# Projection steps between the RWKV chain's products: counts per place, order of the items, and the place of one sigmoid

## What is computed

```python
# per layer
x += 1/2 * g0 * RMSNorm_post(SwiGLU_a(mod0(RMSNorm_pre(x))))
x +=       g1 * RMSNorm_post(HybridMixer(mod1(RMSNorm_pre(x))))
x += 1/2 * g2 * RMSNorm_post(SwiGLU_b(mod2(RMSNorm_pre(x))))

# HybridMixer: h @ w_in gives the columns of three branches and of the merge gates
def rwkv_step(state, inp):                  # 16 heads of 64, forward and backward in time
    sa = einsum("bhij,bhj->bhi", state, a_t)
    state = state * w_t[:, :, None, :] + sa[..., None] * b_t[:, :, None, :] + v_t[..., None] * k_t[:, :, None, :]
    return state, einsum("bhij,bhj->bhi", state, r_t)

def mamba(z, xbc, dt):
    xbc = silu(depthwise_conv_centred(xbc, conv_w) + conv_b)      # 5 taps, 3072 channels
    ...                                                          # chunked scan gives y
    y = y * silu(z)                                              # 2048 channels

def diff_attention(q, k, v): ...
```

## Time and profile before

| what | value |
|---|---|
| median of 3 runs | 2737.57 us (2735.68 to 2737.82) |
| the profiled execution's own time | 2737.22 us |
| its span | 2735.5 us |
| mean granted TensorE clock | 0.993 |
| PE busy | 2620.0 us (96%) |
| DVE busy | 1413.6 us (52%) |
| ACT busy | 499.4 us (18%) |
| POOL busy | 232.0 us (8%) |

### The profile page before, as it was taken

How to read it: one execution, slowest core, us unless ns; L and a number is a source line. 1 busy time by engine, 2 the same in 40 slices (tenths; PEclk the granted TensorE clock), 3 DMA queues, 4 the chain that set the end, 5 groups by cost and what they waited for, 6 DMA issues and landing times.

```text
span 2735.5 us, 66483 instructions
## 1 busy us (share of the span) xinstructions
PE 2620.0 (96%) x30077; PEld 1906.3 (70%) x30077; DVE 1413.6 (52%) x2560; ACT 499.4 (18%) x1016; POOL 232.0 (8%) x372
## 2 busy tenths in 40 slices
PE   6999999999999999999999999999999899999999
PEld 6777877777775555577787778777778745546776
DVE  3552465677775856312035425456787768562001
ACT  1000223122222332100010011322222223221000
POOL 6000102000001101100000010110000011100000
PEclk9999999999999999999999999999999999999999
DMA  9894433322327542484469734423222275424452
GB/s 364 309 337 151 133 117 123 111 83 92 116 80 239 169 168 94 144 291 165 157 242 340 271 128 142 152 91 113 87 83 88 91 253 191 143 96 154 138 168 93
DMA packets 226348, 445.12 MB, mean 163 GB/s; under 512 B 7545, under 2 KB 102327, under 8 KB 226065
## 3 DMA queue, kind: packets, MB, share of 16 engines
q1 hardware_dynamic: 211376, 395.59, 41.5%
q0 software_dynamic: 12960, 38.98, 4.5%
q10 hardware_dynamic: 1728, 6.29, 0.6%
HBM read 422.88 MB, written 17.96 MB: 161 GB/s over the span
## 4 chain that ended last, share of the span: by engine, by line
PE 81%; DVE 11%; ACT 3%; issue 2%; DMA 2%; POOL 1%; DVEq 0%; ACTq 0%; SPq 0%; POOLq 0%
PE ps L1039 79%; DVE scratch L2228 5%; DVE scratch L2231 2%; DVE scratch L2234 1%; DVE gbc L2234 1%; PE ps L1068 1%; DVE scratch L2544 1%; DMA scratch<-in_ada_w 1%; DMA ring<-in_w_in 1%; DMA scratch<-acs_scratch 0%; DMA acs_scratch<-scratch 0%; ACT scratch L2053 0%; ACT scratch L2051 0%; ACT scratch L2200 0%; DVE x L2234 0%
## 5 line engine op out<-in xcount | busy, mean ns | idle before, releaser
L1039 PE MATMUL ps<-hT,ring 64*64 64x256 f32 (+3 forms) x9472 | 1147.9, 367 | 8.3 <-issue 3.1
L1039 PEld LDWEIGHTS ps<-hT,ring 64*64 64x64 f32 (+2 forms) x9472 | 943.0, 160 | 155.9 <-issue 35.8
L1039 PE MATMUL ps<-scratch 64*64 64x32 f32 (+6 forms) x15264 | 846.7, 255 | 56.8 <-DVE scratch L2228 16.1
L1039 PEld LDWEIGHTS ps<-scratch 64*64 64x64 f32 (+2 forms) x15264 | 592.6, 140 | 332.3 <-issue 206.2
L2228 DVE TENSOR_TENSOR scratch<-scratch,ps 128x256 f32<-128x256 f32 (+3 forms) x314 | 155.2, 494 | 661.1 <-ACT scratch L1895 533.1
L1039 PE MATMUL ps<-ring,hT 64*64 64x256 f32 (+2 forms) x2816 | 425.4, 421 | 5.3 <-DVE scratch L2234 2.6
L1039 PEld LDWEIGHTS ps<-ring,hT 64*64 64x64 f32 (+1 forms) x2816 | 228.7, 149 | 143.3 <-issue 116.8
L2228 DVE TENSOR_TENSOR scratch<-scratch 128x512 f32<-128x512 f32 (+4 forms) x426 | 276.1, 648 | 75.4 <-ACTq L2035 31.8
L1039 PE MATMUL ps<-ring,scratch 128*128 128x512 f32 x512 | 234.7, 593 | 0.5
L2234 DVE SCALAR_TENSOR_TENSOR scratch<-scratch,ccol 128x1024 f32<-128x1024 f32 x120 | 154.2, 1285 | 15.2 <-DMA scratch<-in_ada_w 11.3
L1895 ACT ACTIVATE scratch<-ps 128x512 f32<-128x512 f32 x40 | 23.9, 597 | 746.1 <-PE ps L1039 746.1
(11 more groups left out here) (228 smaller groups left out, 1392.8 us busy)
## 6 DMA issues: line engine op xcount, KB each, us to landing
ring<-in_w_in SPq DMA_DIRECT2D x56, 2048.0 KB, 9.0
ring<-in_ffn_w SPq DMA_DIRECT2D x88, 1024.0 KB, 9.0
scratch<-in_ada_w SPq DMA_DIRECT2D x35, 2048.0 KB, 16.2
scratch<-in_ffn_w SPq DMA_DIRECT2D x44, 1024.0 KB, 5.0
ring<-in_w_branch_mamba SPq DMA_DIRECT2D x8, 2048.0 KB, 8.0
scratch<-acs_scratch POOLq DMA_DIRECT2D x24, 512.0 KB, 5.8
scratch<-fill_scratch SPq DMA_DIRECT2D x16, 512.0 KB, 8.7
ring<-in_w_branch_rwkv SPq DMA_DIRECT2D x4, 2048.0 KB, 11.1
```

The lines of the kernel that those rows point to most:

```text
L1039: return pe.matmul(o, lhsT, rhs, start=start, stop=stop)
```

## The change

1. `FILL` has another order. z3 moves from fourth to fifth place, and c1 to c4 each come ahead of a q item that they stood behind; the last three stay.
2. `FILL_PAIR` has new counts. The total is the same 448; the rows' sums are 51, 48, 55, 57, 54, 64, 58 and 61.
3. Convolution 0 belongs to pair 1, not 2. In pair 1 its 16 taps stand otherwise than elsewhere: none before `pair_finish` and none behind the first half, 4 behind the second, 3 in each of four levels. Pair 2 has no taps and no `conv_product`.
4. ACT visits the fill at point `lv` too. At `k3`, if an item ends there, `conv_sigmoid` of the complete convolution goes right behind the item's two copies, ahead of its opens; if not, it stands alone as before.
5. POOL's product for z3 moves from the turn q = 2 to q = 3, one turn later in its loop; the waits for `silu_product` go by the new order (`silu_order`).

```diff
-FILL = [("z", 0), ("z", 1), ("z", 2), ("z", 3), ("c", 0), ("q", 0), ("c", 1), ("q", 1), ("c", 2), ("q", 2),
-        ("c", 3), ("q", 3), ("c", 4), ("c", 5), ("v", 0), ("v", 1)]
+FILL = [("z", 0), ("z", 1), ("z", 2), ("c", 0), ("z", 3), ("c", 1), ("q", 0), ("c", 2), ("q", 1), ("c", 3),
+        ("q", 2), ("c", 4), ("q", 3), ("c", 5), ("v", 0), ("v", 1)]
...
 FILL_POINTS = ("ops", "mid", "lv", "k0", "k1", "k2", "k3", "r0", "u0", "s1", "r1", "u1", "s2", "r2", "u2", "s3", "r3", "u3", "end")
-FILL_PAIR = ((8, 8, 8, 2, 2, 2, 2, 0, 2, 0, 1, 1, 4, 1, 2, 0, 2, 2, 3),
-             (14, 10, 10, 3, 3, 3, 3, 0, 2, 0, 1, 1, 4, 1, 2, 0, 2, 2, 3),
-             (14, 10, 10, 3, 3, 3, 3, 0, 2, 0, 1, 1, 4, 1, 2, 0, 2, 2, 3),
-             (14, 10, 10, 3, 3, 3, 3, 0, 2, 0, 1, 1, 4, 1, 2, 0, 2, 2, 3),
-             (14, 8, 7, 1, 2, 2, 2, 0, 1, 0, 1, 1, 3, 1, 1, 0, 1, 1, 3),
-             (11, 8, 8, 2, 2, 2, 2, 0, 2, 0, 1, 2, 4, 2, 2, 0, 2, 2, 9),
-             (8, 8, 8, 2, 2, 2, 2, 0, 2, 0, 1, 1, 4, 1, 2, 0, 2, 2, 3),
-             (14, 8, 7, 1, 2, 2, 2, 0, 1, 0, 1, 1, 3, 1, 1, 0, 1, 1, 0))
+FILL_PAIR = ((7, 9, 9, 1, 2, 2, 2, 0, 2, 0, 1, 2, 6, 1, 2, 0, 2, 1, 2),
+             (13, 8, 8, 0, 0, 1, 1, 0, 1, 0, 1, 1, 6, 1, 2, 0, 1, 1, 3),
+             (13, 7, 8, 1, 1, 1, 1, 0, 2, 0, 2, 2, 7, 1, 2, 0, 2, 2, 3),
+             (13, 9, 9, 1, 2, 2, 2, 0, 2, 0, 1, 2, 6, 1, 2, 0, 2, 1, 2),
+             (13, 8, 8, 0, 0, 1, 1, 0, 1, 0, 1, 1, 6, 1, 2, 0, 1, 1, 9),
+             (13, 10, 8, 1, 1, 1, 1, 0, 2, 0, 2, 2, 7, 1, 2, 0, 2, 2, 9),
+             (13, 10, 8, 1, 1, 1, 1, 0, 2, 0, 2, 2, 7, 1, 2, 0, 2, 2, 3),
+             (13, 7, 8, 1, 1, 1, 1, 0, 2, 0, 2, 2, 7, 2, 2, 0, 2, 2, 8))
...
-CONV_AT_LEVELS = CONV_SIGMOID = {2: 0, 3: 1, 4: 2, 5: 3, 6: 4, 7: 5}
+CONV_AT_LEVELS = CONV_SIGMOID = {1: 0, 3: 1, 4: 2, 5: 3, 6: 4, 7: 5}
...
-                    if q == 2:
+                    if q == 3:
                         store_product("z", 3)
...
                     act.wait_ge(*fill_evac(l, 2 * i + 2))
+                    if between is not None:
+                        conv_sigmoid(between)
...
                             item_evacuate(u // 2, conv)
                             evacuated_units[0] += 2
+                            conv = None
+                    if conv is not None:
+                        conv_sigmoid(conv)
...
                     if q:
-                        fill_evacuations(q - 1, "k3")
-                        if q - 1 in CONV_SIGMOID:
-                            conv_sigmoid(CONV_SIGMOID[q - 1])
+                        fill_evacuations(q - 1, "lv")
+                        fill_evacuations(q - 1, "k3", CONV_SIGMOID.get(q - 1))
                         fill_evacuations(q - 1, "u0")
...
-                            convolve(2 if d else 4)
+                            convolve((4 if d else 0) if p == 1 else (2 if d else 4))
...
-                            convolve(2)
+                            convolve(3 if p == 1 else 2)
```

More of the change, by code:

```diff
@@ L1975, in fill_evacuate, with item_evacuate @@
                             sigmoid_from_tanh(zsig, silu_sig)
-                def item_evacuate(i):
+                def item_evacuate(i, between):
                     kind, k = FILL[i]
@@ L1983, in item_evacuate @@
                     if kind == "z":
-                        act.wait_ge(*silu_product(l, k))
+                        act.wait_ge(*silu_product(l, silu_order(i)))
                     for r in range(2):
@@ L2009, in conv_sigmoid @@
                     act.wait_ge(*conv_taps(l, 2 * k + 2))
-                    act.wait_ge(*silu_product(l, 4 + k))
+                    act.wait_ge(*silu_product(l, silu_order(FILL.index(("c", k)))))
                     own.step(act.activation(zsig, landing(FILL.index(("c", k))), ACT.Tanh, scale=0.5))
@@ L2014, in _, with fill_evacuations @@
                 evacuated_units = [0]
-                def fill_evacuations(p, point):
+                def fill_evacuations(p, point, conv=None):
                     while evacuated_units[0] < units_filled(p, point):
@@ L2023, in fill_evacuations @@
                         else:
-                            item_evacuate(u // 2)
+                            item_evacuate(u // 2, conv)
                             evacuated_units[0] += 2
+                            conv = None
+                    if conv is not None:
+                        conv_sigmoid(conv)
                 def value_sigmoid(n):
@@ L2095, in pair_body @@
                         fill_evacuations(p, "lv")
-                        conv_sigmoid(CONVS - 1)
+                        fill_evacuations(p, "k3", CONVS - 1)
                         fill_evacuations(p, "end")
@@ L2620, in pair_body @@
                         pair_scale(p - 1)
-                        if p in CONV_AT_LEVELS:
+                        if p in CONV_AT_LEVELS and p > 1:
                             convolve(2)
```

## The result

The changed kernel takes 2761.32 us in the median (2758.33 to 2762.36, 4 runs), the kernel before beside it 2737.07 us (2735.68 to 2737.82, 4 runs). The ratio is 1.0087, with a 95% interval of 1.0074 to 1.0101: slower by 24 us, outside the forecast range. The profiled execution has a span of 2756.6 us against 2735.5, and a mean granted clock of 0.98 against 0.993.

The account below looks back on a forecast made before the run. PE bounds the kernel (81% of the last chain, busy 96%), so only its gaps and clock can change. Terms +23.8 + 1.4 - 19.6 - 9.4 + 0.5 - 2.6 + 10 = +4.1 gave 2741 us, range 2720 to 2754.

Parts of the forecast that it names:

- Levels, uncovered: Pair levels, both layers: missing steps and pair 1's three taps a level leave PE waiting for DVE, +23.8 us.
- Gaps named issue, and the clock behind them: Behind item ends in the pair stages: gaps as many as now, one more half-clock place, +10 us (-8 to +15).
- thin levels take the clock: Rival, slower: granted clock falls to 0.50 in the levels of pairs 1 and 4, +12 us, 2753 us, chance 0.24.
- Sigmoid and chunks: Waits for the sigmoid's multiplication (L2678) and at s2 and u2 (L2231) covered, both layers: -19.6 us, other end -10.
- The tail: Behind pair 7: eight steps cover the 3.18 us norm wait and save 1.5 us of clock, both layers: -9.4 us.
- `mid`, `ops`, z3 and ends of items: Missing `mid` steps +1.4 us, z3's moved product 0; fewer waits for ACT's copies at half and item ends, -2.6 us.
- The rule of the Trainium skill: Rival, faster: instruction fetch mostly hidden, no gap comes of loads, gaps could all close: -33 us, 2704 us, chance 0.04.

Follow-up runs that it names:

- Experiments 5 to 9: Ring loads cut to 64 of 512 columns (5 before, 6 changed), one-column taps (7 changed), both (8 changed, 9 before): 2717.10, 2728.99, 2737.79, 2705.15, 2714.39 us.
- Experiment 3: Changed kernel's code with old item order, counts, convolution places and z3 product turn, leaving only ACT's part: 2729.38 us, ratio 0.9968 to the kernel before.
- experiment 6: Changed kernel with the 16 items' ring loads cut to 64 of 512 columns: 2728.99 us (2720.94 to 2739.71), ratio 0.9971 to the kernel before.
- experiment 8: Changed kernel with small ring loads (64 of 512 columns) and convolution taps on one column: 2705.15 us, ratio 0.9879 to the kernel before.

## Why the prediction was wrong, step by step

**Levels, uncovered (+23.8): right as far as it went.** Where the clock held, the arithmetic of missing steps is exact. Pair 4 of the second layer, at a clock of 1.00, has a level segment of 12.4 us net against 10.7: 1.7, four missing steps of 0.44. With small loads pairs 5 and 6 show 11.56 against 9.8. Pair 1 came to +6.5 a layer (5.8 forecast), its half clock largely hidden in its waits. The waits themselves grew by less than 23.8: those for L2228, now L2232, outside the tail rose from 14.3 to 28.2 us, since slower products fill part of them.

**Gaps named issue, and the clock behind them (+10, ends -8 and +15): this step failed.** I counted one more place of the kind of pair 5's `k0`: pair 5 freed, and two new ones at the `k0` ends. I put these in pairs 1 and 7, but by the list ahead of the prediction they are in pairs 2 and 7. Both fell in both layers. Pair 5 was not freed: with q2 ending at its `mid` the load still lands over its levels, and its fall in the second layer is the longest of all (2061 to 2079). The `mid` ends of pairs 5 and 6, which I named and gave no price, made 4 of the 8 gaps in the levels. All gaps together rose only from 18.8 to 24.0 us, but those in the levels from 5.0 to 14.4, and the lost clock from 9.2 to 44.4. The runs show why: thin levels meet a fall by waits for DVE (pairs 1 and 4) and by a load over them (pair 2; pair 7 by the same sign; in pairs 5 and 6 mixed with waits), and the new table opened one or the other in six pairs of eight. I let each be a rival or a term of its own, and did not see that the same thinning feeds both. Together they make the levels +44.7, some 21 over the waits that were priced, and 21 us is also what PE's busy time grew by. The upper end of the range had room for 13 in all.

**What came out by luck.** Without the clock, the forecast's waits add up to about -1.4 us (23.8 + 1.4 - 19.6 - 6.4 + 0.5 - 2.6 + 1.5), and PE's idle time in the windows changed by -1.2. The parts don't agree so well: waits in the levels are shorter than priced since the half clock fills them, and those for ACT's copies longer.

**The rival "thin levels take the clock" (2753, chance 0.24) named the mechanism and undersized it**, with two pairs at 3 us in each layer. In pairs 1 and 4, where it looked, three of four places fell and lost 10.2 us of clock, most of it hidden in waits. Over the four load-struck pairs 34 us were lost, and for these it had nothing. Experiments 5 to 9 split it.

**Sigmoid and chunks (-19.6): right in kind, and too small.** The chunks fell by 28.3, and by 23.5 (181.1 to 157.6) where loads are small and the place of gaps counts for little; most of the rest is gaps that left the chunks when the c items' ends left `k3`. L2678 and L2231 went from 21.0 us to 3.2. Experiment 3 shows that 7 us of this needed no new table.

**The tail (-9.4): the wait right, the clock not.** The 3.18 us are gone: from pair 7's last chain product to its turn PE took 5.9 us before and takes 6.1 with eight steps (3.5 us) in it, 3.3 less a layer. The stretch at 0.50 behind it is gone too, but gave nothing: from that turn to the first direction products of the next layer it is 929.7 us before and 929.6 now, in the profiled executions. So the tail is -6.6, and the 1.5 us a layer for the clock did not come: something that was not followed up sets the time behind it.

**`mid`, `ops`, z3 and ends of items (+1.4 and -2.6 together): wrong in sign.** The segments of `ops` rose by 7.5, and PE's waits for ACT's copies, which were to shrink, rose from 2.2 to 7.6 us in the two stages. Two places in `ops`, in each layer, make most of its part: PE waits 1.22 us for pair 2's operands, with z3's product moved there, and 1.30 us in pair 3 for the copy of q0, which ends inside `ops`:

```profile
531.92 0.62 PE L1039 MATMUL ps<-stack_i,scratch 64*64 64x64 f32 x14 [1.22 <-DVE scratch L2232]
...
583.19 2.17 PE L1039 MATMUL ps<-hT,ring 64*64 64x256 f32 x36 [1.30 <-ACT scratch L1990]
```

I had 0.75 for the second, and set the first against a saving in pair 1 that didn't come: its `ops` segment is no shorter than before. That z3's product is what delays pair 2 was argued from its place, not tried.

**The rule of the Trainium skill** ("Runtime: NRT & Kernel Launch", "Instruction fetch mechanics": fetching is mostly hidden) got 0.04. The trace agrees that instructions come by a DMA queue of their own while PE works. But in the kernel before, small loads take the gaps from 18.8 us to 1.8 and 20 us of time with them, so "mostly hidden" does not hold here while a 2 MB load has the DMA engines. Where the load is small, it does.

**Open.** Why small products with few steps between lose the clock with no wait to speak of in one place and not in the next. Two stretches alike can differ: pair 4's levels in the changed kernel, with the same waits of 0.69 us, ran at 0.56 in the first layer (651 to 658) and at 1.00 in the second (2003 to 2012). No run tells why. The falls of each kernel are read from one execution, and kernels with thin levels scatter more from run to run (experiment 6: 19 us between ends in ten runs; the kernel before beside it: 10 in 23), so the place of a single short fall proves little; the table by pair, with the same answer in both layers for pairs 1, 2 and 7, is firmer. No run changed only the ends of items, at full loads and with the table's counts.

## What to carry to other kernels

Independent work between the steps of a chain does two jobs: it covers waits, and it keeps PE from short stretches of tiny products that lose the clock. Before such work is taken from a place, ask what the place looks like without it and which transfer starts there, since a short stall can come with several us at half clock. Change the end of a large load and the count of covering steps separately: here the small parts by themselves (sigmoid 7 us, one step to `s2` another 8) gained, and the table made anew lost them again.

## What the runs showed of the hardware

Ring loads of 2 MB that PE never waited for by name, 16 a layer, cost 20 us together in the kernel before, by PE gaps named issue of up to 2.4 us; with each load an eighth of its size one gap of 0.9 us a layer was left. All 8 gaps of 1 us or more there ended 2.4 to 2.6 us after a 16 KB packet of the instruction queue began to move behind full DMA engines. A fall to the 1.2 GHz level came behind such gaps (2.94 us, then 0.57 in the 8 us window), behind waits for DVE of 1.2 and even 0.7 us with nothing else between but small products, and in experiment 8 behind small products with waits of 0.2. A stretch at that level ran on for 3 to 17 us, most of it with PE busy throughout. Behind pair 7 such a stretch of 3.4 us cost nothing that the time shows (929.7 and 929.6 us with and without it).
